# Two halves of the moving operand in one product of 512 columns, for 64 weight tiles

## The reference

```python
proj = u @ w_in                      # q, k, v, x_lru, g_lru, gate_attn, gate_lru
y_attn = attn @ w_branch_attn
y_lru = (hl * gelu(g_lru)) @ w_branch_lru
merged = sigmoid(gate_attn) * y_attn + sigmoid(gate_lru) * y_lru
h = h + rms_norm(merged @ w_out, post)
m = square(relu(rms_norm(h, pre) @ w_mlp_up)) @ w_mlp_down
h = h + rms_norm(m, post)
```

## Time and profile before

| | |
|---|---|
| median of 3 runs | 1193.82 us (1193.74 to 1193.91) |
| profiled execution | 1194.28 us, of which the span of the trace is 1192.5 |
| PE busy | 1053.8 us (88%), 5026 matmuls |
| PEld busy | 725.4 us (61%) |
| DVE busy | 651.7 us (55%) |
| ACT busy | 532.8 us (45%) |
| POOL busy | 693.3 us (58%) |
| granted clock | 0.992 |
| chain that ended last | PE 52%, DMA 31%, DVE 7%, ACT 4%, issue 4% |

### The profile page before, as it was taken

One profiled execution on the slowest core, in us unless ns is written; L12 is line 12 of the kernel. 1 busy time (PEld: TensorE's weight loads), 2 busy tenths in 40 slices (PEclk: granted clock), 3 DMA queues, 4 the chain that ended last, 5 costly groups with the idle time before them and its releaser, 6 DMA issues.

```text
span 1192.5 us, 15197 instructions
## 1 busy us (share of the span) xinstructions
PE 1053.8 (88%) x5026; PEld 725.4 (61%) x5026; DVE 651.7 (55%) x1437; ACT 532.8 (45%) x1301; POOL 693.3 (58%) x433
## 2 busy tenths in 40 slices
PE   7998988888898877877777778999999999999998
PEld 5874544444454322322232224999999997998996
DVE  3577888877586576774774446423455543210212
ACT  5765434433422322323223235546666436554554
POOL 6744544344444434343344343985797886988885
PEclk9999999999999999899999999999999999999999
DMA  7769999999999999999999997773445554556553
GB/s 253 263 242 420 416 421 421 420 421 421 421 420 421 422 421 421 389 423 421 421 421 422 418 420 299 239 240 107 151 159 165 188 177 155 198 178 201 186 179 105
DMA packets 66388, 372.29 MB, mean 312 GB/s; under 512 B 7656, under 2 KB 8784, under 8 KB 33488
## 3 DMA queue, kind: packets, MB, share of 16 engines
q0 software_dynamic: 37152, 268.45, 54.3%
q1 hardware_dynamic: 26656, 97.02, 24.3%
q10 hardware_dynamic: 2512, 5.94, 1.5%
HBM read 369.80 MB, written 1.06 MB: 311 GB/s over the span
## 4 chain that ended last, share of the span: by engine, by line
PE 52%; DMA 31%; DVE 7%; ACT 4%; issue 4%; POOL 1%; ACTq 0%; DVEq 0%; POOLq 0%
DMA arena<-in_peer_uv,idx_all 31%; PE ps L1627 13%; PE ps L1629 12%; PE ps L1628 12%; PE ps L1925 11%; DVE arena L1402 3%; DVE arena L1533 1%; PE ps L1986 1%; ACT prob L761 1%; POOL arena L458 1%; ACT wts L755 1%; ACT gel L748 1%; PE ps L1614 0%; PE ps L1746 0%; PE ps L2001 0%
## 5 line engine op out<-in xcount | busy, mean ns | idle before, releaser
L1925 PE MATMUL ps<-arena,prob 128*128 128x512 f32 x1024 | 475.7, 610 | 119.0 <-ACT prob L761 117.2
L458 POOL DMA_INDIRECT arena<-in_peer_uv,idx_all x254 | 278.9, 1098 | 373.6 <-PE ps L1925 327.8
L442 POOL TENSOR_TENSOR w_hl<-ring,w_hl 128x1024 fp32r<-128x1024 f32 x148 | 370.2, 2518 | 102.8 <-ACT w_hl L549 93.6
L1925 PEld LDWEIGHTS ps<-arena,prob 128*128 128x128 f32 x1024 | 187.8, 192 | 391.2 <-ACT prob L761 198.4
L1402 DVE CUSTOM_DVE_ANT_0 arena<-arena,xn 128x1024 f32<-128x1024 f32 x256 | 312.4, 1225 | 191.6 <-DMA arena<-in_peer_uv,idx_all 187.0
L1627 PE MATMUL ps<-xT,w_hl 128*128 128x256 f32 x760 | 217.8, 287 | 1.7 <-DVE xT L1040 0.6
L1629 PE MATMUL ps<-xT,w_hl 128*128 128x256 f32 x760 | 215.0, 283 | 0.0
L1628 PE MATMUL ps<-xT,w_hl 128*128 128x256 f32 x760 | 215.0, 283 | 0.0
L748 ACT ACTIVATE gel<-acts 128x2 f32<-128x2 f32 (+1 forms) x130 | 26.5, 204 | 402.6 <-DVE acts L1402 402.1
L549 ACT ACTIVATE w_hl<-ring 128x1024 fp32r<-128x1024 f32 x157 | 165.5, 1058 | 89.9 <-PE ps L1629 82.5
L1627 PEld LDWEIGHTS ps<-xT,w_hl 128*128 128x128 f32 x760 | 145.7, 192 | 3.6 <-issue 2.0
(11 more groups left out here) (311 smaller groups left out, 1180.8 us busy)
## 6 DMA issues: line engine op xcount, KB each, us to landing
ring<-in_weights SPq DMA_DIRECT2D x174, 512.0 KB, 3.5
arena<-in_peer_uv,idx_all POOLq DMA_INDIRECT x254
held<-in_weights SPq DMA_DIRECT2D x4, 512.0 KB, 5.8
arena<-in_rg_weights ACTq DMA_DIRECT2D x1, 2048.0 KB, 10.4
x<-in_x SPq DMA_DIRECT2D x2, 512.0 KB, 5.3
bias<-rel_scratch ACTq DMA_DIRECT2D x1, 1024.0 KB, 8.3
arena<-in_subkeys SPq DMA_DIRECT2D x1, 1024.0 KB, 6.0
out_x<-x ACTq DMA_DIRECT2D x4, 256.0 KB, 2.1
```

The lines of the kernel that those rows point to most:

```text
L442: pool.tensor_tensor(pair[:, 1], raw(n), pair[:, 0].bitcast(F32), ALU.subtract).then_inc(w_lo, 1)
L458: pool.indirect_dma_start(uv_slot(n), None, A["peer_uv"], bass.IndirectOffsetOnAxis(idx_all[:, h, c:c + 1], 0))\
L1925: j = pe.matmul(banks(2 + 2 * t + half), diag[:, n % GRING, :], uv_slot(n)[:, D + half * 512:D + (half + 1) * 512], start=(h == 0 and c % ...
```

## The change

For q and k (16 tiles), G (8), the attention branch (8) and the MLP's up products (32), 64 tiles in all, `product` is replaced by `wide_product`. Per chunk it issues one matmul of the high weights with both parts of the operand side by side, 512 columns, and one of the low weights with the high part, 256 columns, into columns 256 to 511. So columns 0 to 255 (`main_half`) hold high x high, columns 256 to 511 (`rest_half`) the other two terms, and the two halves have to be added afterwards. One engine writes the main half to SBUF and DVE adds the rest half from PSUM:

- q and k: ACT writes the main half, DVE adds, and only then `proj_evac` counts. The adds stand in DVE's program between the convolution and the rotations.
- G: DVE copies, then adds.
- Attention branch: DVE copies the main half to `projT[:, m]`, adds the rest half, and multiplies with the gate, now with both operands in SBUF.
- MLP: ACT writes the main half without relu, ahead of its split of tile m+3 instead of behind it; DVE adds the rest half; DVE computes max(h, 0) x h from SBUF into the main half's bank; the two steps after it stay. The up products use banks 0 to 3, and product m waits for `hid_done` of product m-4 instead of m-2; the first turn's products 2 and 3 wait for none.

```diff
+        def wide_bank(f):
+            return banks((f - F_UP) % 4 if f >= F_UP else f % 2)
...
-                evac_proj(F_QK2 + m, projT[:, m, :]).then_inc(proj_evac, 1)
+                evac_proj(F_QK2 + m, projT[:, m, :]).then_inc(qk_main, 1)
...
                 for m in range(16):
+                    if m < 8:
+                        act.wait_ge(w_used, i * 16 + (W_MLP + m + 1))
+                        act.activation(hid[:, m, :], main_half(F_UP + m), ACT.Identity).then_inc(hid_main, 1)
                     if not isinstance(i, int):
                         split_hi(W_MLP + m + AHEAD, i, 16)
                     elif W_MLP + 16 * i + m + AHEAD < W_END:
                         split_hi(W_MLP + 16 * i + m + AHEAD)
                     if m < 8:
-                        act.wait_ge(w_used, i * 16 + (W_MLP + m + 1))
-                        act.activation(hid[:, m, :], banks((F_UP + m) % 2)[:, 0:SEQ], ACT.Relu).then_inc(proj_evac, 1)
                         act.wait_ge(hid_sq, i * 8 + (m + 1))
...
+            for m in range(16):
+                dve.wait_ge(qk_main, m + 1)
+                dve.tensor_tensor(projT[:, m, :], rest_half(F_QK2 + m), projT[:, m, :],
+                                  ALU.add).then_inc(proj_evac, 1)
...
-                dve.tensor_copy(projT[:, 24 + m, :], banks((F_G2 + m) % 2)[:, 0:SEQ]).then_inc(g_evac, 1)
+                dve.tensor_copy(projT[:, 24 + m, :], main_half(F_G2 + m)).then_inc(g_main, 1)
+                dve.wait_ge(g_main, m + 1)
+                dve.tensor_tensor(projT[:, 24 + m, :], rest_half(F_G2 + m), projT[:, 24 + m, :],
+                                  ALU.add).then_inc(g_evac, 1)
...
-                dve.tensor_tensor(projT[:, 32 + m, :], banks((F_BA + m) % 2)[:, 0:SEQ], projT[:, 32 + m, :],
+                dve.tensor_copy(projT[:, m, :], main_half(F_BA + m)).then_inc(attn_main, 1)
+                dve.wait_ge(attn_main, 2 * m + 1)
+                dve.tensor_tensor(projT[:, m, :], rest_half(F_BA + m), projT[:, m, :], ALU.add).then_inc(attn_main, 1)
+                dve.wait_ge(attn_main, 2 * m + 2)
+                dve.tensor_tensor(projT[:, 32 + m, :], projT[:, m, :], projT[:, 32 + m, :],
                                   ALU.mult).then_inc(gated_evac, 1)
...
-                    up = banks((F_UP + m) % 2)[:, 0:SEQ]
-                    dve.wait_ge(proj_evac, i * 8 + (F_BA + m + 1))
-                    dve.tensor_tensor(up, up, hid[:, m, :], ALU.mult).then_inc(hid_sq, 1)
+                    up = main_half(F_UP + m)
+                    dve.wait_ge(hid_main, i * 8 + (m + 1))
+                    dve.tensor_tensor(hid[:, m, :], rest_half(F_UP + m), hid[:, m, :], ALU.add).then_inc(hid_sum, 1)
+                    dve.wait_ge(hid_sum, i * 8 + (m + 1))
+                    dve.scalar_tensor_tensor(out=up, in0=hid[:, m, :], scalar=0.0, in1=hid[:, m, :],
+                                             op0=ALU.max, op1=ALU.mult).then_inc(hid_sq, 1)
...
+                for c in chunks:
+                    if fresh is not None:
+                        fresh(c)
+                    pe.matmul(wide_bank(f).rearrange("p (a n) -> p a n", a=2), w[:, 0, c, :], src[:, :, c, :],
+                              start=c == 0, stop=False)
+                    i = pe.matmul(rest_half(f), w[:, 1, c, :], src[:, 0, c, :], start=False, stop=c == NC_ - 1)
...
-                    product(F_UP + m, turn + m, xTc, lambda: pe.wait_ge(hid_done, 8 * i + m - 1))
+                    wide_product(F_UP + m, turn + m, xT,
+                                 (lambda: pe.wait_ge(hid_done, 8 * i + m - 3)) if i or m > 3 else (lambda: None))
```

More of the change, by code:

```diff
@@ L358, in raw, with main_half, rest_half @@
             return at.rearrange("p (c n) -> p c n", n=P)
+        def main_half(f):
+            return wide_bank(f)[:, 0:SEQ]
+        def rest_half(f):
+            return wide_bank(f)[:, SEQ:2 * SEQ]
+        def wide_bank(f):
+            return banks((f - F_UP) % 4 if f >= F_UP else f % 2)
         def scores_of(h):
@@ L984, in mlp_turn @@
                     if m < 8:
-                        act.wait_ge(w_used, i * 16 + (W_MLP + m + 1))
-                        act.activation(hid[:, m, :], banks((F_UP + m) % 2)[:, 0:SEQ], ACT.Relu).then_inc(proj_evac, 1)
                         act.wait_ge(hid_sq, i * 8 + (m + 1))
-                        act.activation(yT[:, 0, m, :], banks((F_UP + m) % 2)[:, 0:SEQ], ACT.Identity).then_inc(hid_hi, 1)
+                        act.activation(yT[:, 0, m, :], main_half(F_UP + m), ACT.Identity).then_inc(hid_hi, 1)
             with act.Fori(0, 3) as i:
@@ L1643, in product, with wide_product @@
                     i.then_inc(w_used, 1)
+            def wide_product(f, n, src, wait, fresh=None, chunks=range(NC_)):
+                w = weight(n)
+                wait()
+                for c in chunks:
[4 more added lines that the diff above has]
+                    i = pe.matmul(rest_half(f), w[:, 1, c, :], src[:, 0, c, :], start=False, stop=c == NC_ - 1)
+                if c == NC_ - 1:
+                    i.then_inc(w_used, 1)
             xTc = lambda c: parts(xT, c, slice(None))
@@ L1650, in chunk @@
                     if c % 2 == 0:
-                        pe.wait_ge(xT_dve, 4 * k + (2 + c // 4 + 1 if k == 2 else 2 * (c // 4) + 2))
+                        pe.wait_ge(xT_dve, 4 * k + 2 + c // 4 + 1)
                     return xTc(c)
                 return chunk
-            yTc = lambda c: parts(yT, c, slice(None))
             evacuated = lambda f, turn=None: (lambda: pe.wait_ge(
@@ L1972, in _ @@
                 f = F_QK2 + m
-                product(f, W_QK2 + m, xTc,
-                        evacuated(f) if m >= 2 else (lambda: pe.wait_ge(conv_step, 3 * (8 + m - 1))))
+                wide_product(f, W_QK2 + m, xT,
+                             evacuated(f) if m >= 2 else (lambda: pe.wait_ge(conv_step, 3 * (8 + m - 1))))
             pe.wait_ge(conv_step, 24)
@@ L1990, in g_product @@
             def g_product(m):
-                product(F_G2 + m, W_G2 + m, xTc,
-                        evacuated(F_G2 + m) if m < 2 else (lambda: pe.wait_ge(g_evac, m - 1)))
+                wide_product(F_G2 + m, W_G2 + m, xT,
+                             evacuated(F_G2 + m) if m < 2 else (lambda: pe.wait_ge(g_evac, m - 1)))
             for m in range(6):
@@ L2031, in _ @@
             for m in range(8):
-                product(F_BA + m, W_BA + m, yTc,
-                        evacuated(F_BA + m) if m < 2 else (lambda: pe.wait_ge(gated_evac, m - 1)))
+                wide_product(F_BA + m, W_BA + m, yT,
+                             evacuated(F_BA + m) if m < 2 else (lambda: pe.wait_ge(gated_evac, m - 1)))
             def fresh_hl(c):
@@ L2055, in _ @@
                 for m in range(2):
-                    product(F_UP + m, W_MLP + m, fresh_xTc(3),
-                            lambda: pe.wait_ge(proj_evac, F_UP + m - 17), chunks=chunks)
+                    wide_product(F_UP + m, W_MLP + m, xT, lambda: pe.wait_ge(proj_evac, F_UP + m - 17),
+                                 lambda c: pe.wait_ge(xT_dve, 4 * 3 + 2 * (c // 4) + 2), chunks)
             for i in range(4):
```

2 lines of the change are left out of this document (added).

## The result

The kernel after takes 1200.82 us (median of 8, 1196.32 to 1202.89) against 1193.87 for the kernel before on the same chip (1193.0 to 1194.62): ratio 1.0051, 95% interval 1.0038 to 1.0064. It is 0.5% slower, and lies outside the forecast range. Three of the eight times lie from 1196.32 to 1197.68 us and five from 1200.71 to 1202.89, and the profiled execution is one of the five (1202.83 us, span 1201.0), so that what the other three did differently stays open. The profiled execution of before took 1194.28.

The account below looks back on a forecast made before the run. From 785 us on, PE's own pace plus a few hand-overs was taken to bound the kernel. Terms -1.4 (q and k), -0.85 (G), +4.6 (attention branch) and -3.9 (MLP) sum to -1.55: 1192.3 us, range 1187.2 to 1196.0.

Parts of the forecast that it names:

- The attention branch, +4.6: Attention branch: DVE's two-SBUF operations and POOL's splits exclude each other, last multiply at 28.4 against 23.86 us, +4.6.
- the granted clock should stay: Attention branch: PE idles 1 to 2 us at a time, clock stays, since 700 to 750 us has 18% idle at 1.00.
- Nothing ahead of the branch: Wait of PE ahead of the attention branch: a change of 0 was forecast.
- The pair, 0.3467: All 64 products: a 512- and a 256-column matmul take 0.3467 us instead of 0.3600, ceiling 6.8 us saved.
- Term -1.7: q and k: 16 products save 0.107 us each, 1.7 us in all.
- term -3.4: MLP: 32 up products save 0.107 us each, 3.4 us in all.
- The MLP "holds": MLP up products: POOL needs 2.63 of 2.77 us a product, so it keeps up; net -3.9 for the MLP.
- Rotations hidden: After q and k: DVE's first rotation ends 8 us after the products, the second waits for its transfer till 9.6.
- bank wait -0.6: MLP's first turn: product 2's 0.6 us wait for the square of product 0 goes with four banks.
- Rivals: Attention branch doesn't stall, 1187.6 (half stalls 0.32); its products take four steps in a row, 1197.5 (0.10); pair not shorter, 1199.0 (0.07).
- rival 2: Attention branch: every product goes through all four steps in a row, 3.84 us; branch +9.9, kernel 1197.5; chance 0.10.
- -2.4 to +1.8: Whole kernel: the forecast's change by its bounds, 1191.4 to 1195.6 us; chance 0.51.

Follow-up runs that it names:

- the branch alone: Only the attention branch's 8 tiles changed as in the change, against the kernel before: 1201.05 us, ratio 1.0058.
- product 7 alone: Change without its attention branch, low-part splits moved ahead (1191.06); ACT splits the weight tile ahead of its evacuation in MLP product 7 only: 1190.89 us, 0.9974.

## Why the prediction was wrong

- **The attention branch, +4.6: right in mechanism, short by the clock.** The walk, the prediction's step-by-step account of the branch, gave 28.4 us; 27.38 were measured where the clock stayed whole, 28.53 with the branch alone, 29.81 in the change. That the total of the walk came so near is in part luck: of its four pauses, before products 3, 4 and 7 and before the BL branch, the change shows those before 4 and BL, the branch alone those before 3 and BL. The failed step is "the granted clock should stay". It rested on the busy share of the earlier trace rows, and didn't ask how long a single pause lasts. The last hand-over is one pause of 4.33 us, not the 1 to 2 us that I expected, and the two halvings cost 2.3 us in the BL branch and an estimated 1.3 to 1.6 in this one (25.19 against 23.86 in the kernel before with and without the 24 copies, 25.35 against 23.76 in the change without its attention branch, as it is and with the splits moved).
- **Nothing ahead of the branch: wrong, +2.7.** This is the second failed step. The walk started with the branch as the earlier trace rows shows it, and never asked what PE's first matmul waits for, the splits behind eight scans, which are operations on two SBUF inputs like those of the earlier trace rows, and which were on time only because one of them fell into a pause of POOL. The change put 24 operations, each with its wait, on DVE ahead of them, and 24 copies of one column in the kernel before had the same effect. No row of before could have given this number; that the chain had no slack could be read (PE's start at 932.16, the splits' end at 929.63 + 2.47 = 932.10).
- **The pair, 0.3467: right in G, in most of the branch and in five products of the MLP's first turn, 0.353 in q and k, in the first turn's other three and in the later turns.** The products of q and k save 16 x 0.053 = 0.85 us instead of 1.7, an up product of turns 2 to 4 0.053 instead of 0.107. Term -1.7 measured -1.1, term -3.4 measured about -2.0 (-2.6 with the bank wait).
- **The MLP "holds": right but for the end, +1.1.** PE waits there for POOL's split, one of the prediction's own signs of being wrong. The forecast counted POOL's time per product, 2.63 of 2.77, and did not follow the splits to the last products, where the last four tiles are used for one row tile first, so that each is needed 1.36 us after the one before (six starts of 0.2267) and not 2.72. That the splits come late there because ACT's split now stands behind its evacuation is argued and not shown: the one run that could have shown it, product 7 alone, left 0.99 of the 1.12 us.
- **Rotations hidden, recurrence gates +0.3, G -0.85, bank wait -0.6: as forecast.**
- **Rivals.** None of the three happened. A closed chain in the manner of rival 2 (3.84 us a product) came not in the branch but in the MLP of an experiment, at 4.20 and by way of ACT.
- **The bounds.** The terms with their own ranges give -1.65 to +1.65 us, not -2.4 to +1.8; the result lies far above either.

The terms don't add up alone: the branch costs 7.2 us on top of the kernel before and 5.1 on top of the rest of the change, since its pauses and halved clock meet others.

The change without its attention branch, with the low-part splits moved ahead (1191.06) or with PSUM inputs for four scans (1191.06), is faster than the kernel before by 0.24 and 0.26% (0.9966 to 0.9986 and 0.9965 to 0.9983).

## What to carry to other kernels

Before making PE faster in a stage, look at what PE's first matmul there waits for, and how late that is, even where the profile shows no wait. Count DVE operations with two SBUF inputs against another engine's SBUF work as one queue, and look for a loop through it; an operand in PSUM takes an operation out. A pause of PE costs itself and, when it is long, the clock behind it: in the second block behind each of the seven pauses of 3.07 us or more between starts, and behind none of those of 2.58 us and less; in the first block behind some of those of 2.8 us.

## What the runs showed of the hardware

- DVE operations with two SBUF inputs wait out POOL's split whether they write to SBUF or PSUM, scans and scalar_tensor_tensor too (0.42 becomes up to 2.64, a scan of 0.66 to 0.69 becomes 2.83); with one input in PSUM they take 0.42 and 0.60 beside the same splits. That is what the Trainium skill, "SBUF — State Buffer", section "SBUF: two separate sides", says of such pairs, and the runs agree.
- The number of instructions ahead on DVE moved an instruction's start by 0.36 us, and through the scans the kernel by 4.7 us, in both directions.
- A 512-column matmul in alternation with a 256-column one takes 0.347 or 0.353 us a pair, the same instructions in the same place; what decides stays open.
- The granted clock fell to its lower level behind every one of the seven pauses of 3.07 us or longer between starts from 750 us on, over six kernels. Behind one pause of 2.8 us at 703, the same in all traces, it halved in five and stayed whole in fourteen.
